# Expert tiles for overflow picks spread among the tiles of the fixed experts

## What is computed

```python
def hier_moe(h, wgc, bgc, wgf, bgf, w1, w3, w2):
    ...
    pg = jax.nn.softmax(jnp.dot(t, wgc, preferred_element_type=f32) + bgc.astype(f32), axis=-1)
    gw, gi = lax.top_k(pg, 1)
    ...
    tv, ti = lax.top_k(jax.nn.softmax(fs, axis=-1), TOP_K_IN_GROUP)
    ...
    eid = gi * EXPERTS_PER_GROUP + ti
    ...
    a = jnp.einsum('td,edf->tef', t, w1)
    c = jnp.einsum('td,edf->tef', t, w3)
    act = jax.nn.silu(a) * c * gates[:, :, None].astype(t.dtype)
    y = jnp.einsum('tef,efd->td', act, w2)
```

## Time and profile before

| | us |
|---|---|
| median of 3 runs | 2746.53 |
| lowest, highest | 2746.37, 2746.92 |
| the profiled execution | 2741.5 |
| its span | 2739.5 |

### The profile page before, as it was taken

One profiled execution on the slowest core, in us unless ns is written; L12 is line 12 of the kernel. 1 busy time (PEld: TensorE's weight loads), 2 busy tenths in 40 slices (PEclk: granted clock), 3 DMA queues, 4 the chain that ended last, 5 costly groups with the idle time before them and its releaser, 6 DMA issues. The chain is left out here.

```text
span 2739.5 us, 35274 instructions
## 1 busy us (share of the span) xinstructions
PE 2681.4 (98%) x12337; PEld 2093.5 (76%) x12337; DVE 1772.4 (65%) x2575; ACT 1090.2 (40%) x1892; POOL 1597.1 (58%) x979
## 2 busy tenths in 40 slices
PE   8999999999999999999999989999999999999998
PEld 6777778888887777788888877778777677787675
DVE  6787755444127787654444749886777588777775
ACT  3844423222025544432221011644556415545554
POOL 5754466666676744486666765576236555772263
PEclk9999999999999999999999989999999999999999
DMA  4332222333332312223333322236896232357951
GB/s 156 86 84 62 63 86 83 96 96 100 92 93 85 100 62 70 62 85 94 98 97 126 109 90 85 70 100 241 303 354 209 69 97 73 94 209 295 352 181 64
DMA packets 89673, 340.29 MB, mean 124 GB/s; under 512 B 21568, under 2 KB 24384, under 8 KB 80064
## 3 DMA queue, kind: packets, MB, share of 16 engines
q1 hardware_dynamic: 66592, 298.02, 32.9%
q0 software_dynamic: 19008, 26.28, 3.7%
q10 hardware_dynamic: 3936, 14.16, 1.4%
HBM read 368.77 MB, written 33.55 MB: 147 GB/s over the span
## 5 line engine op out<-in xcount | busy, mean ns | idle before, releaser
L188 POOL TENSOR_TENSOR wl<-ring,wh 128x1024 fp32r<-128x1024 f32 x317 | 784.0, 2473 | 26.4
L186 POOL TENSOR_SCALAR wh<-ring 128x1024 fp32r<-128x1024 f32 x317 | 352.0, 1111 | 724.1 <-PE ps L265 516.5
L263 PE MATMUL ps<-xh,wh 128*128 128x512 f32 x1592 | 633.8, 398 | 14.0 <-DVE xl L1421 11.8
L264 PE MATMUL ps<-xl,wh 128*128 128x512 f32 x1592 | 621.2, 390 | 0.0
L265 PE MATMUL ps<-xh,wl 128*128 128x512 f32 x1592 | 621.2, 390 | 0.0
L263 PEld LDWEIGHTS ps<-xh,wh 128*128 128x128 f32 x1592 | 299.6, 188 | 94.2 <-issue 12.6
L265 PEld LDWEIGHTS ps<-xh,wl 128*128 128x128 f32 x1592 | 299.6, 188 | 64.2
L264 PEld LDWEIGHTS ps<-xl,wh 128*128 128x128 f32 x1592 | 300.0, 188 | 60.8 <-issue 1.0
L1673 DVE SCALAR_TENSOR_TENSOR taps<-ps,par,taps 128x511 f32<-128x511 f32 x192 | 143.8, 749 | 232.1 <-ACT taps L1391 216.3
L3271 DVE TENSOR_TENSOR ew_l<-ew,ew_h 128x1024 fp32r<-128x1024 f32 x184 | 214.1, 1217 | 5.2 <-ACT ew_h L2794 5.1
L2794 ACT ACTIVATE ew_h<-ew 128x1024 fp32r<-128x1024 f32 x184 | 180.6, 1050 | 13.3 <-DMA ew<-in_eu 9.3
(11 more groups left out here) (628 smaller groups left out, 5326.0 us busy)
## 6 DMA issues: line engine op xcount, KB each, us to landing
ring<-in_w SPq DMA_DIRECT2D x343, 512.0 KB, 3.6
ew<-in_eu SPq DMA_DIRECT2D x32, 2048.0 KB, 12.5
ew<-in_ed SPq DMA_DIRECT2D x32, 1024.0 KB, 11.4
xrows<-xr ACTq DMA_DIRECT2D x8, 512.0 KB, 2.8
yrows<-xr ACTq DMA_DIRECT2D x8, 512.0 KB, 3.8
yg<-yrows SPq DMA_DIRECT2D x8, 512.0 KB, 5.1
z<-in_x SPq DMA_DIRECT2D x4, 512.0 KB, 5.7
join_in<-in_ln ACTq DMA_DIRECT2D x1, 2048.0 KB, 9.4
```

Source lines behind the costliest of these rows:

```text
L186: nc.gpsimd.tensor_scalar(hi, raw, 1.0, 0.0, ALU.mult, ALU.add).then_inc(sem["w_hi"], 1)
L188: nc.gpsimd.tensor_tensor(lo, raw, hi, ALU.subtract).then_inc(sem["w_split"], 1)
L263: nc.tensor.matmul(out, wh, xh, start=first, stop=False, **kw)
L264: nc.tensor.matmul(out, wh, xl, start=False, stop=False, **kw)
```

## The change

The seven spare tiles leave the end of the loop. They are now tiles 4, 7, 10, 13, 16, 19 and 22 (`is_spare`), each between two fixed ones, and the fixed experts keep their order in the other places; tile 21 is the last fixed one. All spares use buffer 1. Every test of the form j < EXPERTS becomes one of is_spare(j), and a spare's number is spares_until(j). A scatter waits for the one before it if either of the two is a spare's: 12 such waits per layer instead of 6.

```diff
+def is_spare(j):
+
+    return j > EW_BUFS and j % EW_BUFS == 1
+
+
+def spares_until(j):
+
+    return sum(is_spare(i) for i in range(j))
+
+
 def held(j):
 
-    return j % GROUPS * (EXPERTS // GROUPS) + j // GROUPS if j < EXPERTS else j
+    fixed = j - spares_until(j)
+    return EXPERTS + spares_until(j) if is_spare(j) else fixed % GROUPS * (EXPERTS // GROUPS) + fixed // GROUPS
...
-                    for j in range(EXPERTS - EW_BUFS + 1):
-                        if j + EW_BUFS < EXPERTS:
+                    for j in range(TILES - EW_BUFS + 1):
+                        if j + EW_BUFS < TILES and not is_spare(j + EW_BUFS):
                             sp.wait_ge(sem["up_mm"], at("up_mm", UP_PARTS * (j + 1)))
                             load_up(j + EW_BUFS)
-                        if j:
+                        if j and not is_spare(j - 1 + EW_BUFS):
                             sp.wait_ge(sem["dn_mm"], at("dn_mm", j))
                             load_down(j - 1 + EW_BUFS)
...
-                        if j >= EXPERTS:
+                        if j and (is_spare(j) or is_spare(j - 1)):
                             g.wait_ge(sem[f"y_out{(j - 1) % 2}"], at(f"y_out{(j - 1) % 2}", 16 * ((j - 1) // 2 + 1)))
...
-                        if EXPERTS <= j + EW_BUFS < TILES:
+                        if j + EW_BUFS < TILES and is_spare(j + EW_BUFS):
                             spare_up(j + EW_BUFS)
                         if j + 3 < TILES:
                             gather_rows(j + 3)
-                        if EXPERTS <= j + EW_BUFS - 1 < TILES:
+                        if j and j + EW_BUFS - 1 < TILES and is_spare(j + EW_BUFS - 1):
                             spare_down(j + EW_BUFS - 1)
                         if j:
                             scatter_rows(j - 1)
...
```

More of the change, by code:

```diff
@@ L1759 @@
         **{f"xg_in{n}": 16 * turns_of(TILES, n, 2) for n in range(2)}, **{f"y_out{n}": 16 * turns_of(TILES - 1, n, 2) for n in range(2)},
-        **{f"ew_{w}{n}": 16 * turns_of(EXPERTS, n, EW_BUFS) for w in ("up", "dn") for n in range(EW_BUFS)},
+        **{f"ew_{w}{n}": 16 * sum(not is_spare(j) for j in range(n, TILES, EW_BUFS)) for w in ("up", "dn") for n in range(EW_BUFS)},
         **{f"es_{w}{n}": 16 * turns_of(TILES - EXPERTS, n, 2) for w in ("ua", "ub", "dn") for n in range(2)},
@@ L2087, in spare_up @@
                     def spare_up(j):
-                        k, last = j - EXPERTS, (layer + 1) * ROWS_E - 1
+                        k, last = spares_until(j), (layer + 1) * ROWS_E - 1
                         for half, name in enumerate((f"es_ua{k % 2}", f"es_ub{k % 2}")):
@@ L2532, in expert_down @@
                         pe.wait_ge(sem["hactt"], at("hactt", j + 1))
-                        if j < EXPERTS:
+                        if not is_spare(j):
                             pe.wait_ge(sem[f"ew_dn{b}"], at(f"ew_dn{b}", 16 * (j // EW_BUFS + 1)))
                         else:
-                            k = j - EXPERTS
+                            k = spares_until(j)
                             pe.wait_ge(sem[f"es_dn{k % 2}"], at(f"es_dn{k % 2}", 16 * (k // 2 + 1)))
@@ L2784, in weights_high @@
                         b = j % EW_BUFS
-                        if j < EXPERTS:
+                        if not is_spare(j):
                             act.wait_ge(sem[f"ew_up{b}"], at(f"ew_up{b}", 16 * (j // EW_BUFS + 1)))
                         for u in parts:
-                            if j >= EXPERTS and u % 2 == 0:
-                                k, name = j - EXPERTS, ("es_ub" if u else "es_ua") + str(j % 2)
+                            if is_spare(j) and u % 2 == 0:
+                                k = spares_until(j)
+                                name = ("es_ub" if u else "es_ua") + str(k % 2)
                                 act.wait_ge(sem[name], at(name, 16 * (k // 2 + 1)))
```

## The result

| | before | changed |
|---|---|---|
| median of 6 runs, us | 2746.45 | 2760.32 |
| lowest, highest | 2745.39, 2746.92 | 2756.28, 2769.75 |
| the profiled execution | 2741.5 | 2757.98 |
| its span | 2739.5 | 2756.0 |

The account below looks back on a forecast made before the run. TensorE, busy 98% of the span, was taken as the bound, with DMA full but not late. End +7.2 and start +4.0 us, other terms 0, gave +11.2 on the 2746.5 median: 2757.7 us, range 2750.5 to 2765.

Parts of the forecast that it names:

- three signs of being wrong: Last scatter landing in under 5 us, early steps unchanged, or VectorE waiting for a scatter before tile 10.
- its marks: Expected profile signs, among them TensorE idle above 6 us before the last transposes and later steps of 10.02 to 10.1.
- End of the loop: Tile 21's scatter, now full, lands later with nothing hiding it: +3.6 us in layer 0, about the same in layer 1.
- Start of the loop: Tile 4's spare load runs beside tile 3's load and delays it and TensorE: +2.0 us per layer, between 0 and 6.0.
- Rival (a): Loop start: the spare load takes only time tile 4's load took before, so +7.2 us, 2753.7 us; chance 0.15.
- rival (b): Loop start: queues share evenly, all 2048 KB ahead of tile 3's load's end, +6.0 us per layer, 2765.7 us; chance 0.08.
- The measured 0.22 us for each shared us: Loop start: slowdown seen in layer 1's last fixed load beside spare halves, applied to 9.8 us shared, giving 2.2.
- Spare loads 0: Expert loops: the spares' own weight loads land in time, charged nothing; bounds 0 to +1 us per layer.
- scatter waits 0: GpSimd in the loops: 12 scatter waits per layer instead of 6 cost nothing; upper bound 3 us per layer.
- Relief 0: Fixed-expert steps and loop start: less full DMA could give back 1.8 us per layer at most; counted as 0.
- Rival (d): Loops: relief of DMA pays for the end, fixed steps 10.02 us, +2.0 us in all, 2748.5 us; chance 0.14.
- Clock 0: End of layer 0: longer idle changes TensorE's lower-clock stretch, from 1.5 us gain to 1 us more; taken as 0.

Follow-up runs that it names:

- e1_tail: Changed kernel with spares at tiles 15 to 20 and 22, fixed expert 15 in place 21, old order up to tile 14; ratio to the kernel before 1.0032.
- e5_perm: Changed kernel with row-holding spares moved to tiles 13 and 16 and empty ones at 4, 7 and 10; ratio to the kernel before 1.0063.
- e6_hold: Changed kernel, but GpSimd issues tile 4's spare load only when tile 3's up load has landed; ratio to the kernel before 1.0067.
- e10_shift_b: Kernel before, but in layer 0 SyncE reads 1024 columns of 128 rows of yrows and waits before the read back; ratio to the kernel before 1.0015.
- e4_split: Changed kernel with the two weight splits of layer 0's loop in turns 8 and 11 instead of 10 and 12; ratio to the kernel before 1.0046.
- e2_start: Changed kernel with spares at 4, 7, 10, 13, 16, 21 and 22, so the last scatter is empty again; ratio to the kernel before 1.0015.
- e8_relief: Changed kernel with spares at 3, 7, 10, 13, 16, 21, 22, those with rows at 7 and 10, splits in turns 8 and 11; ratio to the kernel before 1.0005.

## Why the prediction was right, and where it was not

The total fits better than its terms, and that is in part luck. The ends were put 1.5 us too high, the late split of 1.1 us was not in the sum, and neither was the clock. The first six runs of the changed kernel make it 15.7 us slower by the ratio, the six later ones 11.0, on either side of the 13.9 between the medians of the first table; the forecast was 11.2. None of its three signs of being wrong came. Two of its marks were missed: TensorE's idle time stayed under 6 us, and not every step after the third is 10.02 to 10.1.

*End of the loop* (+3.6 per layer). Right in mechanism and near in size. The scatter lands in 6.02 and 5.90 us, +3.2 in each layer, inside the bounds of 2.8 and 4.5; e1_tail has 5.95 by itself. The term took 7.3 us less 0.9 for the busy queue, which is 6.4. The net change of the stage is 2.71 and 2.95, because from the scatter's landing to the transposes it takes 9.4 us instead of 9.85 (layer 0). That is also why TensorE's idle time is 5.5 us and not above 6. The prediction gave tile 21 71 rows in layer 0; its scatter there has 144 packets like that of layer 1, 73 of them of a row each, so it is 73 in both, which changes nothing.

*Start of the loop* (+2.0 per layer). Right in layer 0: the second and third steps make 10.98 + 12.04 = 23.02 where they made 10.19 + 10.86 = 21.05, so +1.97, and tile 3's load took 1.9 us more. e5_perm (the start is back without the real load) and e6_hold (the load is in time when nothing runs beside it) show the cause. In layer 1 the sum fits, +2.04, but this execution can't prove it: a stretch at the lower clock lies on it, and such a stretch makes the same 11.89 us with the old loads in e10_shift_b. Executions without one give 1.8 (the changed kernel again), 1.6 (e4_split) and 1.0 (e2_start). The load is worth 1 to 1.8 us there, so the term of 2.0 was somewhat large. The step that should have become 12.9 us is 12.04, because 0.8 of the 2 us fall into the step before it. Rival (a), a free start, falls with this.

*The queues share evenly* (rival (b), and the rule of the Trainium skill quoted with it). Wrong here: 1.9 us more against 6.0. The two halves beside the load slowed it by a third of what even shares would. The measured 0.22 us for each shared us was the better guide: 9.8 x 0.22 = 2.2.

*Spare loads 0, scatter waits 0.* The second of these failed. Its direct form held: in the changed kernel no copy waits for a scatter. But behind the wait the prediction had named only the next gather and scatter. GpSimd's queue also carries the splits of layer 1's weights, and the wait pushed one of them beside VectorE's low parts: +1.05 us in the twelfth step of layer 0, 1.26 in e2_start, and a part of the 8 us in e5_perm. Layer 1, in whose loop no such split runs, has no such step. The spare loads that came late behind the split cost TensorE nothing in the profiled execution and 0.24 us of waiting in the second one, so that zero was near.

*Relief 0.* Right. With DMA at 0.83 the fixed steps are 10.04 to 10.12 us, as with 0.96. Full DMA engines had cost TensorE nothing that could come back, and e8_relief, which takes the relief and leaves out the prices, is not faster. Rival (d) falls with it.

*Clock 0.* This failed too, and is the largest miss: 4.3 us in the body of layer 1 and 1.3 in the rest of the two profiles, and at most some 7 us over all executions, by the means of the granted clock. Why the changed kernel gets the lower clock more often stays open. The prediction looked at the clock in one place, the end of layer 0, and not at what happens 130 to 250 us later, where nothing is changed. Of the 16.5 us, by stages and rows: ends 5.7, start of layer 0 2.0, the late split 1.1, loop 1 2.0 (load or clock), clock 5.5, and 0.2 in single steps and the part ahead of the loops.

## What to carry to other kernels

Full DMA engines beside a TensorE at 98% are no reserve: ask which instruction waits for a transfer before moving transfers apart, and leave an empty or small transfer at the place where everything waits for the last one. When a wait goes on an in-order queue, go through everything that stands behind it for the next two or three turns, other layers' work included, and compute from that when each of them runs and what it then runs beside. For differences below 0.3%, compare stages cut at the same instructions, and before giving a difference in untouched code to the change, profile both kernels more than once and shift that code by a few us with the rest as it was.

## What the runs showed that was not expected

Layer 1's body, the same instructions with the same queues, took 315.7 to 315.9 us in five profiled executions, 319.0 to 320.3 in seven and 314.7 in one, and the difference lies in short stretches in which TensorE's granted clock is 1.2 instead of 2.4 GHz although in two of the three windows TensorE was busy for 7.00 of 7.00 us. A kernel that differs from the one before only by a delay of 2 us, in a place where TensorE is idle anyway, had the long body; whether the delay or the execution made it is open.

GpSimd's tensor instructions beside VectorE's ew_l made four parts take 6.01 to 7.44 us instead of 4.62, and TensorE waited 0.8 to 1.9 us behind them. A full accumulating scatter lands in 6 us where the DMA engines are quiet, an empty one in 2.7 to 2.8.
